# Two projections, two norms and the upward projections as one interleaved phase, in a two-block transformer on one core

## The reference

```python
# end of _layer (first block)
return x + jnp.einsum('bsd,de->bse', merged.astype(x.dtype), w_out)     # 1024 x 1024
# start of second_block
h = rms_norm(x, attn_norm_g[i])
z = h @ w_in[i]                                   # 1024 x 1952
# start of mla_group: z[..., 0:256] is q_lat, z[..., 256:384] is kv_lat
q = (rms_norm(q_lat, q_lat_g) @ w_uq)             # 256 x 768
kv = (rms_norm(kv_lat, kv_lat_g) @ w_ukv)         # 128 x 1024
```

## Time and profile before

| | |
|---|---|
| Median of three runs | 3191.02 us (3188.89 to 3194.04) |
| Profiled execution, first to last instruction | 3186.9 us |
| TensorE busy | 2674.4 us (84%) |
| VectorE, ScalarE, GpSimd busy | 1277.0, 989.5, 224.0 us |
| From the first matmul of `out1` to the last copy of `up_kv` | 385.8 us (1278.9 to 1664.7) |

### The profile page before, as it was taken

How to read it: one execution, slowest core, us unless ns; L and a number is a source line. 1 busy time by engine, 2 the same in 40 slices (tenths; PEclk the granted TensorE clock), 3 DMA queues, 4 the chain that set the end, 5 groups by cost and what they waited for, 6 DMA issues and landing times. The chain is left out here.

```text
span 3186.9 us, 39198 instructions
## 1 busy us (share of the span) xinstructions
PE 2674.4 (84%) x15182; PEld 2302.9 (72%) x15182; DVE 1277.0 (40%) x1832; ACT 989.5 (31%) x1573; POOL 224.0 (7%) x259
## 2 busy tenths in 40 slices
PE   5969999987989648959954888766999999799669
PEld 4859999976878546748843767655788888678469
DVE  4533444424655344231126757432333333233333
ACT  3322222214554431030124656422222222222221
POOL 0002222201000000000002222000000000000000
PEclk9989999998999869979966999887999999899879
DMA  2232222122311233332144111133222222344422
GB/s 93 99 90 69 60 59 62 39 63 78 88 53 44 77 119 119 116 131 90 54 142 128 41 40 34 66 107 125 54 79 68 70 79 66 115 170 159 161 94 92
DMA packets 256538, 278.54 MB, mean 87 GB/s; under 512 B 56036, under 2 KB 198500, under 8 KB 256392
## 3 DMA queue, kind: packets, MB, share of 16 engines
q1 hardware_dynamic: 255336, 274.45, 27.4%
q10 hardware_dynamic: 1056, 2.10, 0.2%
HBM read 199.27 MB, written 77.22 MB: 87 GB/s over the span
## 5 line engine op out<-in xcount | busy, mean ns | idle before, releaser
L395 PE MATMUL ffn_up_acc<-xn_hi,ffn_w_hi 128*128 128x512 f32 x704 | 217.8, 391 | 3.6 <-PEq L39 3.6
L395 PE MATMUL ffn_up_acc<-xn_lo,ffn_w_hi 128*128 128x512 f32 x704 | 217.3, 390 | 0.0
L395 PE MATMUL ffn_up_acc<-xn_hi,ffn_w_lo 128*128 128x512 f32 x704 | 217.3, 390 | 0.0
L1717 PE MATMUL delta_acc<-delta_w_hi,xn_hi 128*128 128x256 f32 x640 | 191.0, 298 | 2.9 <-DVE delta_w_lo L1671 2.9
L1719 PE MATMUL delta_acc<-delta_w_hi,xn_lo 128*128 128x256 f32 x640 | 180.6, 282 | 0.0
L1718 PE MATMUL delta_acc<-delta_w_lo,xn_hi 128*128 128x256 f32 x640 | 180.4, 282 | 0.0
L261 PE MATMUL norm_t<-ident,norm_xn 128*128 128x128 f32 x256 | 57.2, 399 | 127.1 <-DVE norm_xn L238 127.1
L2107 PE MATMUL ffn_down_acc<-ffn_down_hi 128*128 128x512 f32 x352 | 139.1, 395 | 25.2 <-DVE ffn_down_lo L2092 25.2
L395 PEld LDWEIGHTS ffn_up_acc<-xn_hi,ffn_w_hi 128*128 128x128 f32 x704 | 132.6, 189 | 31.2 <-DMA gather_o<-scratch_o_diff 3.8
L395 PEld LDWEIGHTS ffn_up_acc<-xn_lo,ffn_w_hi 128*128 128x128 f32 x704 | 132.7, 188 | 27.6
L395 PEld LDWEIGHTS ffn_up_acc<-xn_hi,ffn_w_lo 128*128 128x128 f32 x704 | 132.5, 188 | 27.6
(11 more groups left out here) (403 smaller groups left out, 6526.1 us busy)
## 6 DMA issues: line engine op xcount, KB each, us to landing
ffn_down_raw<-scratch_act_t SPq DMA_DIRECT2D x44, 512.0 KB, 3.5
norm_x<-scratch_x SPq DMA_DIRECT2D x24, 512.0 KB, 6.8
ffn_w_raw<-in_w_gate SPq DMA_DIRECT2D x22, 512.0 KB, 4.5
ffn_w_raw<-in_w_up SPq DMA_DIRECT2D x22, 512.0 KB, 5.7
scratch_act_t<-ffn_up_silu SPq DMA_DIRECT2D x22, 512.0 KB, 3.2
ffn_down_raw<-in_w_down SPq DMA_DIRECT2D x44, 256.0 KB, 3.7
delta_w_raw<-in_w_in SPq DMA_DIRECT2D x20, 512.0 KB, 4.0
scratch_projected<-delta_out SPq DMA_DIRECT2D x80, 128.0 KB, 1.7
```

The source lines that it names most:

```text
L395: last = nc.tensor.matmul(out[:, cols], weight[:, k, ch], part[:, k, cols], start=(k == 0 and first), stop=(k == kt - 1 and weight is w_lo))
L1717: nc.tensor.matmul(acc, self.hi[:, k, tok], w_hi, start=(k == 0), stop=False, skip_group_check=True)
```

## The change

The six phases become one, `trunk`, of eight stages stepped by `trunk_plan`. Results go to DRAM as before, but the norms take their input from SBUF. In the first half of the output projection ScalarE squares each tile as it is finished; in the second half the whole chain of a tile (residual, squares, inverse root by GpSimd's power, scale, 8 transposes, `hi` and `lo`) runs two tiles behind the matmuls. The normed tile overwrites the merged tile `m_hi`, `m_lo` of the same tokens. The first 512 columns of the input projection hold the latents; their norm and turn run three tiles behind in the same way. The input projection is cut in widths 512, 512, 512, 416 in place of 4 x 488. All seven weight chunks pass through one ring, the splits placed after the third and fifth tile. One PSUM tile, `turn`, serves all transposes, and `acc` has four. The upward projections take four pieces a token tile: two of 384 and two of 512 columns. The whole is written out without loops.

```diff
--- before.py
+++ after.py
@@ -2893,6 +2893,639 @@
+class WeightRing:
...
+    def load(self, sp, i, h):
+        if i:
+            sp.wait_ge(self.lo_done[h], i)
+        kp, width, source = self.chunks[i][h]
+        sp.dma_start(self.part(self.raw[h], i, h).rearrange("p (k n) -> p k n", n=width),
+                     source.rearrange("(k p) n -> p k n", p=P)).then_inc(self.loaded[h], 16)
...
+    def split_hi(self, act, i, h):
+        act.wait_ge(self.loaded[h], 16 * (i + 1))
+        if i >= 2:
+            slots, key = self.ended[i - 2]
+            slots.wait_filled(act, key)
+        self.nc.scalar.activation(self.part(self.hi[i % 2][:, h], i, h), self.part(self.raw[h], i, h), ACT.Copy
+                                  ).then_inc(self.hi_done[h], 1)
...
+    def sync(self, sp):
+        self.load(sp, 0, 0)
+        self.load(sp, 0, 1)
+        for i, h in self.walk():
+            if i + 1 < len(self.chunks):
+                self.load(sp, i + 1, h)
+            yield
...
+class NormScale:
...
+    def gpsimd(self, pool):
+        o, pooled = self.o, self.o.nc.gpsimd
+        pooled.memset(o.half[:], -0.5).then_inc(o.half_set, 1)
+        for m in range(TT):
+            pool.wait_ge(o.left_squared, m + 1)
+            pooled.tensor_scalar(o.mean[:, m, 0:1], o.total[:, m, 0:1], 1.0 / D, EPS, ALU.mult, ALU.add).then_inc(o.left_meaned, 1)
+            yield
+        pool.wait_ge(o.half_set, 1)
+        for m in range(TT):
+            pool.wait_ge(o.right_squared, m + 1)
+            pool.wait_ge(o.left_meaned, m + 1)
+            pooled.tensor_scalar(o.mean[:, m, 1:2], o.total[:, m, 1:2], 1.0 / D, o.mean[:, m, 0:1], ALU.mult, ALU.add
+                                 ).then_inc(o.right_meaned, 1)
+            pool.wait_ge(o.right_meaned, m + 1)
+            pooled.tensor_tensor(o.inverse[:, m:m + 1], o.mean[:, m, 1:2], o.half[:], ALU.pow).then_inc(o.inverted, 1)
+            yield
...
+    def scalar(self, act):
+        o, nc = self.o, self.o.nc
+        def square(m, half, x, squared):
+            o.acc.wait_read(act, ("out", half, m))
+            if m >= 2 and half == 1:
+                o.turn.wait_filled(act, ("norm", m - 2))
+            if m >= 2 and half == 0:
+                act.wait_ge(squared, m - 1)
+            nc.scalar.activation(o.xn[m % 2][:, half * HALF:(half + 1) * HALF], x, ACT.Square,
+                                 accum_out=o.total[:, m, half:half + 1]).then_inc(squared, 1)
+        for m in range(TT):
+            square(m, 0, o.left[:, m, :], o.left_squared)
+            yield
+        for m in range(TT):
+            square(m, 1, o.right[m % o.DEEP][:], o.right_squared)
+            yield
...
+    def vector(self, dve):
+        o, nc = self.o, self.o.nc
+        for m in range(TT):
+            yield
+        dve.wait_ge(o.gain_in, 16)
+        dve.wait_ge(o.left_squared, TT)
+        for m in range(TT):
+            dve.wait_ge(o.inverted, m + 1)
+            if m >= 2:
+                o.turn.wait_filled(dve, ("norm", m - 2))
+            for half, x in enumerate((o.left[:, m, :], o.right[m % o.DEEP][:])):
+                cols = slice(half * HALF, (half + 1) * HALF)
+                last = nc.vector.scalar_tensor_tensor(o.xn[m % 2][:, cols], x, o.inverse[:, m:m + 1], o.gain_row[:, cols],
+                                                      ALU.mult, ALU.mult)
+            last.then_inc(o.scaled, 1)
+            yield
...
+class NormTurn:
...
+    def scalar(self, act):
+        o = self.o
+        for m in range(TT):
+            o.turn.wait_filled(act, ("norm", m))
+            o.acc.wait_filled(act, ("out", 1, m))
+            o.nc.scalar.activation(o.hi[:, :, tile_of(m)], o.turn.tile(("norm", m))[:], ACT.Copy).then_inc(o.hi_done, 1)
+            yield
...
+    def tensor(self, pe):
+        o = self.o
+        for m in range(TT):
+            pe.wait_ge(o.scaled, m + 1)
+            o.turn.wait_free(pe, ("norm", m))
+            for k in range(8):
+                last = o.nc.tensor.transpose(o.turn.tile(("norm", m))[:, k, :], o.xn[m % 2][:, k * P:(k + 1) * P], o.c["ident"][:])
+            o.turn.fill(last, ("norm", m))
+            yield
...
+class Outputs:
...
+    def evacuate(self, eng, key, width, on_act):
+        r = self.number[key]
+        self.acc.wait_filled(eng, key)
+        if r >= self.N:
+            eng.wait_ge(self.stored[r % self.N], 16 * (r // self.N))
+        if on_act:
+            done = self.nc.scalar.activation(self.tile(key)[:, 0:width], self.acc.tile(key)[:, 0:width], ACT.Copy)
+        else:
+            done = self.nc.vector.tensor_copy(self.tile(key)[:, 0:width], self.acc.tile(key)[:, 0:width])
+        self.acc.free(done, key)
...
+class InProject:
...
+    def evacuations(self, eng, on_act):
+        for i, m in self.walk():
+            if (m % 2 == 0) == on_act:
+                key = ("in", i, m)
+                if self.latent and self.outputs.number[key] - self.outputs.N in range(TT):
+                    eng.wait_ge(self.latent.scaled, self.outputs.number[key] - self.outputs.N + 1)
+                self.outputs.evacuate(eng, key, self.widths[i], on_act)
+            yield
...
+    def tensor(self, pe):
+        o = self.o
+        for i, m in self.walk():
+            key, chunk = ("in", i, m), self.first_chunk + i
+            if m == 0:
+                for h in range(2):
+                    o.ring.wait_split(pe, chunk, h)
+            if i == 0:
+                o.wait_parts(pe, m)
+            o.acc.wait_free(pe, key)
+            last = token_products(o.nc, o.acc.tile(key)[:, 0:self.widths[i]], o.hi, o.lo, tile_of(m), o.ring, chunk, 8)
+            o.acc.fill(last, key)
+            yield
...
+class LatentScale:
...
+    def gpsimd(self, pool):
+        l, pooled = self.l, self.l.o.nc.gpsimd
+        pooled.memset(l.half[:], -0.5).then_inc(l.half_set, 1)
+        pool.wait_ge(l.half_set, 1)
+        for m in range(TT):
+            pool.wait_ge(l.squared, 2 * (m + 1))
+            for g, (c0, c1) in enumerate(l.GROUPS):
+                pooled.tensor_scalar(l.mean[:, m, g:g + 1], l.total[:, m, g:g + 1], 1.0 / (c1 - c0), EPS, ALU.mult, ALU.add
+                                     ).then_inc(l.meaned, 1)
+            pool.wait_ge(l.meaned, 2 * (m + 1))
+            pooled.tensor_tensor(l.inverse[:, m], l.mean[:, m], l.half[:], ALU.pow).then_inc(l.inverted, 1)
+            yield
...
+    def scalar(self, act):
+        l = self.l
+        for m in range(TT):
+            key = ("in", 0, m)
+            l.o.acc.wait_read(act, key)
+            if m:
+                act.wait_ge(l.squared, 2 * m)
+            for g, (c0, c1) in enumerate(l.GROUPS):
+                l.o.nc.scalar.activation(l.square[:, c0:c1], l.outputs.tile(key)[:, c0:c1], ACT.Square,
+                                         accum_out=l.total[:, m, g:g + 1]).then_inc(l.squared, 1)
+            yield
...
+    def vector(self, dve):
+        l = self.l
+        dve.wait_ge(l.gain_in, 32)
+        for m in range(TT):
+            key = ("in", 0, m)
+            dve.wait_ge(l.inverted, m + 1)
+            l.o.acc.wait_read(dve, key)
+            if m >= 3:
+                l.o.turn.wait_filled(dve, ("latent", m - 3))
+            for g, (c0, c1) in enumerate(l.GROUPS):
+                last = l.o.nc.vector.scalar_tensor_tensor(l.xn[m % 3][:, c0:c1], l.outputs.tile(key)[:, c0:c1], l.inverse[:, m, g:g + 1],
+                                                          l.gain_row[:, c0:c1], ALU.mult, ALU.mult)
+            last.then_inc(l.scaled, 1)
+            yield
...
+class UpProject:
...
+    PIECES = ((0, 0, 384), (0, 384, 384), (1, 0, HALF), (1, HALF, HALF))
...
+    def tensor(self, pe):
+        l, ring = self.l, self.l.o.ring
+        for m in range(TT):
+            l.o.turn.wait_read(pe, ("latent", m))
+            for key, (which, c0, w) in zip(self.keys(m), self.PIECES):
+                if m == 0 and key[2] % 2 == 0:
+                    ring.wait_split(pe, self.chunk, which)
+                l.o.acc.wait_free(pe, key)
+                out, n = l.o.acc.tile(key)[:, 0:w], 2 - which
+                w_hi, w_lo = ring.weights(self.chunk, which)
+                for k in range(n):
+                    tile, cols = (slice(None), 2 * which + k, tile_of(m)), slice(c0, c0 + w)
+                    l.o.nc.tensor.matmul(out, l.hi[tile], w_hi[:, k, cols], start=(k == 0), stop=False)
+                    l.o.nc.tensor.matmul(out, l.hi[tile], w_lo[:, k, cols], start=False, stop=False)
+                    last = l.o.nc.tensor.matmul(out, l.lo[tile], w_hi[:, k, cols], start=False, stop=(k == n - 1))
+                l.o.acc.fill(last, key)
+            yield
...
+def trunk_plan():
+    ring, out, scale, turn, into, l_scale, l_turn, up = range(8)
+    plan = [ring, ring]
+    for m in range(TT):
+        plan += [out, scale]
+        plan += [ring] * (m in (2, 4))
+    for m in range(TT):
+        plan += [out]
+        plan += [turn] * (m >= 2) + [scale]
```

(77 more changed lines are left out.)

269 lines of the change are left out of this document (added).

## The result

The changed kernel takes 3100.94 us (median of four runs, 3093.77 to 3102.56) where the one before took 3192.53 us beside it (3188.89 to 3194.33). The ratio is 0.9719, with a 95% interval of 0.9707 to 0.973: 91.6 us less. The forecast was 3105.8 us, with a range of 3097 to 3130.

The account below looks back on a forecast made before the run. TensorE was taken as the bound in both projections, with serial latency and a lowered clock in the gaps. Terms summed to 300.6 us in place of 385.8, a gain of 85.2, so 3105.8 us, range 3097 to 3130.

Parts of the forecast that it names:

- Steps 1, 3: Output projection, same 384 matmuls and cold start, 89.7 us; input projection in 512- and 416-column matmuls, 166.7 us.
- Steps 2, 4: Turns between matmuls: eight of 8 transposes, 8.7 us; eight latent turns of 3 transposes, 4.0 us.
- Step 5: Weight splits in VectorE's queue while latents are normed make TensorE wait: 1.8 us, between 0 and 4.
- Steps 6, 7: Upward projections, their copies waiting for stores, 29.0 us; last copy behind the last matmul, 0.7 us.
- rival B: Upward stage is bound by its stores and keeps its old 43.1 us: 14.1 us more, 3120 us; chance 0.11.
- The clock: TensorE's clock in the new stretch is 1.00 after the first few microseconds.
- Rival A: Norm round trip sets the pace, latents' trip over 5.9 us in every tile: 24 us, so 3130 us; chance 0.11.
- Rival C: Stops at turns and upward pieces lower TensorE's clock to 1.2 GHz: slower than before, 3236 us in one case; chance 0.05.

Follow-up runs that it names:

- Run 7: Changed kernel with the input projection cut in the old widths, 4 x 488 columns; 3105.66 us, ratio 0.9733.
- Run 8: Changed kernel with two PSUM tiles for the turns, and first matmuls waiting only for their own half of the weights; 3097.43 us, ratio 0.9716.
- Run 10: Changed kernel with two output buffers instead of four for the copies of the input and upward stages; 3116.96 us, ratio 0.9783.
- run 4: Changed kernel without lag: each tile turned right behind its own matmuls, two and three tiles earlier; 3197.75 us, ratio 1.004.
- run 3: Kernel before with only output projection and second norm fused; input projection, latent norm and upward projections stay separate phases; 3165.83 us, ratio 0.9937.
- run 1: Changed kernel with the second norm's eight tiles scaled and turned in a row after the output projection, still from SBUF; 3126.9 us, ratio 0.9815.

## Why the prediction was right, step by step

| step | predicted us | measured us |
|---|---|---|
| 1 and 2, output projection and its turns; 3 and 4, input projection and the latents' | 269.1 | 266.8 |
| 5, waits at the turns | 1.8 | 1.66 |
| 6 and 7, upward stage and last copy | 29.7 | 29.0 |
| together | 300.6 | 297.5 |

The measured first row is 1550.58 (first upward matmul) less 1282.11, less the waits of 1.66. Of the 4.9 us between forecast and median, 3.1 are this stretch; the rest is run to run.

**Steps 1, 3.** As predicted: the output projection kept its cold start (0.97 in the first row of after), and the 416-column matmuls, never seen before, are (1550.01 - 1547.76) / 12 = 0.1875 us apart, against 0.187 from the line between 384 and 512. Run 7 tests the step from the other side: the old widths cost 4.5 us in the stretch, where the prices give 768 x 0.2215 - 166.7 = 3.4.

**Steps 2, 4 are the ones mis-sized**, by 2.9 us together. I charged a turn its duration in the row, 1.09 us. That duration runs from the first start to the last end and so counts the drain of the pipeline, in which the next matmul already runs. From start to start it costs 0.87 us (the next matmul at 1345.15 begins before the turn ends at 1345.40). Eight of them, and eight of 0.35 instead of 0.5 us, make 9.8 in place of 12.7. With the other two terms as predicted (89.7 + 166.7 + 9.8 = 266.2) the first row of the table is met within 0.6 us.

**Step 5.** The mechanism was named rightly. Two waits came where a split of VectorE stood ahead of a latent's `lo`: 0.60 and 0.64 us, I had said 0.9. In the changed kernel's VectorE queue:

```profile
1399.42 2.28 DVE L2948 TENSOR_TENSOR trunk_ring_lo<-trunk_ring_raw,trunk_ring_hi 128x2048 fp32r<-128x2048 f32 x1
1401.62 0.55 DVE L3416 TENSOR_TENSOR trunk_latent_lo<-trunk_turn,trunk_latent_hi 128x384 fp32r<-128x384 f32 x1
...
1402.32 0.52 PE L3427 MATMUL trunk_turn<-ident,trunk_latent_xn 128*128 128x128 f32 x3 [0.60 <-DVE trunk_latent_lo L3416]
```

The third, 0.42 us at the last output turn, I had not seen. There `lo` of the turn before stands in VectorE's queue behind the first latent, and that one waits for a load that the prediction left out, the latents' gain, which SyncE issued only at 1384.13:

```profile
1387.35 0.75 DVE L3375 SCALAR_TENSOR_TENSOR trunk_latent_xn<-trunk_out,trunk_latent_inverse,trunk_latent_gain 128x256 f32<-128x256 f32 x2 [6.10 <-DMA trunk_latent_gain<-in_kv_lat_norm_g]
1388.02 1.22 DVE L3203 TENSOR_TENSOR merged_lo<-trunk_turn,merged_hi 128x1024 fp32r<-128x1024 f32 x1
...
1389.38 1.07 PE L3213 MATMUL trunk_turn<-ident,trunk_xn 128*128 128x128 f32 x8 [0.42 <-DVE merged_lo L3203]
```

Run 8, with a second PSUM tile for the turns, has none of the three. Loading the gain earlier was not tried.

**Steps 6, 7: the size right, the reason wrong.** I took the stage as paced by its stores, 0.905 us a piece. It is paced by TensorE: busy 20.00 of 20.00 us in the last row of after, and the only wait for a store in the stage is one of 1.3 us, of ScalarE. 384-column matmuls are 0.1765 us apart here and those of 512 columns 0.233, so 96 x 0.1765 + 48 x 0.233 = 28.1 us, and the last copy follows. That this comes near 32 x 0.905 = 29.0 is chance. In `up_kv` every piece was 256 KB and had 3 matmuls, 0.70 us of TensorE; now two such pieces follow two of 192 KB and six matmuls each, 0.88 us of TensorE a piece on average (28.1 / 32). Run 10 shows how far the stores are: two buffers bring the pace to 44.2 / 32 = 1.38 us, four leave them hidden. So rival B fell because four buffers suffice at this pace, not because of the pace that I had borrowed.

**The clock.** 0.97 in the first stretch, then 1.00, as predicted. Rival A fell too: the latent's trip, from the end of its matmuls at 1388.96 to the scaled values at 1392.79, took 3.8 us and with a latent's `lo` of 0.55 us 4.4, the sum of the prediction, where 5.9 were to be had. GpSimd's power, a guess from 8 and 16 columns, took what the line said:

```profile
L3350 POOL TENSOR_TENSOR trunk_latent_inverse<-trunk_latent_mean,trunk_latent_half 128x2 f32<-128x2 f32 x8 | 5.6, 694 | 0.7
...
L3133 POOL TENSOR_TENSOR trunk_inverse<-trunk_mean,trunk_half 128x1 f32<-128x1 f32 x8 | 4.4, 546 | 0.7
```

0.69 and 0.55 us, against 0.7 and 0.55.

Rival C was given 0.05 and did not come: the clock is 1.00 behind the cold start, and no wait in the stretch is over 0.64 us. But its description was better than my argument against it: run 4 takes only the distance of the turns away and lands at 3197.75 us. The prediction should have said that the clock holds as long as the waits are short, and that this rests on the lag.

**Where the gain comes from.** Taken out of the changed kernel one at a time: the overlap of the turns is worth 28.2 us (some of it the one PSUM tile of the serial version), the boundary ahead of the upward stage 11.0, the widths 4.5. Taken alone, output projection with norm brings 19 us. What is left of the 88.3 (the latents' part, the boundary ahead of the input projection with its cold start) was not run by itself, and parts that share a wait needn't add up: run 3 shows one, in which the weights' load takes over the gap.

## What to carry to other kernels

Price a fusion by where its latency will be hidden: a trip of 4 to 5.6 us through four engines cost TensorE nothing at two tiles of lag, 1.3 us a tile at half a tile, and with no lag 4.0 us plus some 2 us of half clock behind each wait, together more than the whole gain. When one part of a gap is hidden, look for what is late next (here the weights), since the gap closes only when all of it has moved. Price small inserts between matmuls from start to start, not by their duration.

## What the runs showed that I had not expected

- The clock falls for short idleness too, and comes back fast: behind one wait of 4.17 us TensorE ran at 0.51 for 5.5 us; behind waits of up to 1.43 us with matmuls between them it stayed at 1.00. Each of the sixteen waits of run 4, 4.0 us on average, so cost about 35 / 16 = 2.2 us on top of itself, some 0.2 of it not the clock.
- Matmuls of the same width are not equally far apart everywhere: 512 columns 0.227 us in the projections and 0.233 in the upward stage, 384 columns 0.173 in `up_q` and 0.1765 in the fused stage. What makes the difference was not tried.
- One PSUM tile for all turns cost only 1.66 us in 297.5, although it couples the transposes with two copies in other engines. Where turns follow each other without matmuls between, it cost 2.46 us a turn (run 1).
